# Two decoder blocks of two layers each: layer loops written out, one weight queue through the program, norm weights loaded once

## What is computed

```python
for l in range(2):                                    # first_block, "A"
    h = rmsnorm(x, g_mix[l])
    (cq, ckv, kr, aq, ak, av, qi, ki, wi, rq, rk, rv, rg) = split(h @ w_in[l])
    ...                                               # latent, sparse and retention attention
    x = x + concatenate([o_a, o_b, o_c]) @ w_out[l]
    x = x + square(relu(rmsnorm(x, g_mlp[l]) @ w_ff1[l])) @ w_ff2[l]
x = rmsnorm(x, g_final)
for i in range(2):                                    # second_block, "B"
    (...) = split(rmsnorm_2(h, ln_mix[i]) @ w_in[i])
    ...                                               # delta rule, sparse and stick-breaking attention
    h = h + mix @ w_out[i]
    h = h + conv_ffn(rmsnorm_2(h, ln_ffn[i]), w_up[i], ffn_conv[i], w_down[i])
    gate = sigmoid(rmsnorm_2(h, ln_ple[i]) @ w_ple_gate[i])
    h = h + gate * rmsnorm_2(p[i] @ w_ple[i], ple_norm[i])
return rmsnorm_2(h, ln_final)
```

## Time and profile before

| | |
|---|---|
| time, median of 3 runs | 3295.99 us |
| runs | 3292.2, 3295.99, 3296.8 us |
| span of the profiled execution | 3298.4 us (its own time outside the profiler is not given) |
| TensorE busy | 3144.2 us, 95% |
| VectorE, ScalarE, GpSimd busy | 55%, 39%, 12% |
| weights read | 234 MB, 72 GB/s over the span |

### The profile page before, as it was taken

How to read it: one execution, slowest core, us unless ns; L and a number is a source line. 1 busy time by engine, 2 the same in 40 slices (tenths; PEclk the granted TensorE clock), 3 DMA queues, 4 the chain that set the end, 5 groups by cost and what they waited for, 6 DMA issues and landing times. The chain is left out here.

```text
span 3298.4 us, 48870 instructions
## 1 busy us (share of the span) xinstructions
PE 3144.2 (95%) x19216; PEld 2651.6 (80%) x19216; DVE 1812.1 (55%) x3220; ACT 1302.5 (39%) x2692; POOL 391.2 (12%) x374
## 2 busy tenths in 40 slices
PE   8999999999999999979999999999899999999996
PEld 6878788877878888868888878888788878788885
DVE  4875443425865424337566457474475565574744
ACT  4454432334354413233374333233443653332324
POOL 1031000001040000001213302010004034010100
PEclk9999999999999999989999999999999999999998
DMA  4111222212202222132100122222222000222230
GB/s 169 55 52 39 90 91 101 90 69 91 74 1 77 90 99 93 51 105 104 65 1 2 40 83 99 91 101 87 73 99 85 1 2 28 83 93 93 93 110 35
DMA packets 37342, 239.55 MB, mean 73 GB/s; under 512 B 4464, under 2 KB 5232, under 8 KB 15088
## 3 DMA queue, kind: packets, MB, share of 16 engines
q1 hardware_dynamic: 36528, 234.21, 20.1%
q10 hardware_dynamic: 576, 2.10, 0.2%
HBM read 234.19 MB, written 2.10 MB: 72 GB/s over the span
## 5 line engine op out<-in xcount | busy, mean ns | idle before, releaser
L265 PE MATMUL ps<-b_hl,bff_whl 128*128 128x512 f32 x704 | 274.1, 389 | 3.1 <-DVE b_hl L667 3.1
L267 PE MATMUL ps<-b_hl,bff_whl 128*128 128x512 f32 x704 | 273.9, 389 | 0.0
L266 PE MATMUL ps<-b_hl,bff_whl 128*128 128x512 f32 x704 | 273.9, 389 | 0.0
L248 DVE SCALAR_TENSOR_TENSOR bff_whl<-ring,b_cols,bff_whl 128x512 fp32r<-128x512 f32 (+1 forms) x224 | 153.2, 745 | 197.3 <-ACT bff_whl L235 197.1
L245 DVE TENSOR_TENSOR aff_whl<-ring,aff_whl 128x512 fp32r<-128x512 f32 x160 | 99.8, 685 | 222.8 <-ACT aff_whl L233 222.7
L235 ACT ACTIVATE bff_whl<-ring,b_cols 128x512 fp32r<-128x512 f32 (+1 forms) x224 | 136.6, 682 | 176.4 <-PE ps L267 176.4
L266 PE MATMUL ps<-aff_whl,a_u 128*128 128x512 f32 x512 | 204.3, 399 | 0.0
L265 PE MATMUL ps<-a_hl,aff_whl 128*128 128x512 f32 x512 | 199.5, 390 | 3.1 <-DVE a_hl L667 3.1
L265 PE MATMUL ps<-aff_whl,a_u 128*128 128x512 f32 x512 | 201.7, 394 | 0.0
L267 PE MATMUL ps<-aff_whl,a_u 128*128 128x512 f32 x512 | 200.7, 392 | 0.0
L267 PE MATMUL ps<-a_hl,aff_whl 128*128 128x512 f32 x512 | 199.2, 389 | 0.0
(11 more groups left out here) (524 smaller groups left out, 7746.5 us busy)
## 6 DMA issues: line engine op xcount, KB each, us to landing
ring<-in_a_w_ff SPq DMA_DIRECT2D x64, 1024.0 KB, 4.6
ring<-in_b_w_up SPq DMA_DIRECT2D x32, 1024.0 KB, 4.7
ring<-in_a_w_in SPq DMA_DIRECT2D x16, 1024.0 KB, 5.9
ring<-in_b_w_down SPq DMA_DIRECT2D x16, 1024.0 KB, 4.6
ring<-in_b_w_in_att SPq DMA_DIRECT2D x12, 1024.0 KB, 4.7
ring<-in_b_w_up SPq DMA_DIRECT2D x16, 768.0 KB, 4.0
ring<-in_b_w_in_conv SPq DMA_DIRECT2D x12, 768.0 KB, 4.2
ring<-in_a_w_out SPq DMA_DIRECT2D x8, 1024.0 KB, 4.8
```

Of the source, the lines that this page charges most:

```text
L248: self.c.nc.vector.scalar_tensor_tensor(out=self.part(j, 1, k), in0=src[:, k, :], scalar=g[:, row + k:row + k + 1], in1=self.part(j, 0, k) ...
L265: nc.tensor.matmul(bank, sh, mh, start=start, stop=False)
L266: nc.tensor.matmul(bank, sh, ml, start=False, stop=False)
L267: return nc.tensor.matmul(bank, sl, mh, start=False, stop=stop)
```

## The change

Both loops are written out: each layer is a call of `first_layer` or `second_layer` with a constant l, and every tile's name carries the layer's tag. `start_layer` and `end_layer` go. `queue_layer` appends all chunks of the four layers to one queue, whose addresses are constants, and the four slots' semaphores count through the program; `may_load` bounds how far SP may load: in A up to the third chunk of B, since the fourth slot holds the final gain (`c.ring` is then that slot), in B to the end. So the last stage of a layer loads the first four chunks of the next one (three from A to B). `end_weights` clears the five semaphores once, at the end, with no barrier. The norm gains of both A layers are loaded once, and so are the columns and rows of both B layers (one DMA for the columns and one per layer for the rows); only `g_ret` is still loaded in each A layer, and nothing in that stage waits for it but SP at its end. The 40 idle transposes at the end of `aff` and of `LayerTail` go. In `LayerTail` ScalarE's final squares are placed between the last sigmoids. In the last norm of all, ScalarE's squares are left out (nobody reads them). The stages themselves stay as they are. The core of the diff:

```diff
+    def queue_layer(self, weights, drams, prefix, l):
+        at = {}
         for name, chunks in weights:
             for k, kt, n, w in chunks:
-                self.queue.append((drams[prefix + name], (k, kt, n, w)))
-                self.offsets.append(at.get(name, 0))
...
+                o = at.get(name, 0)
+                self.queue.append((drams[prefix + name][l:l + 1, :, o:o + kt * w], (k, kt, n, w)))
+                at[name] = o + kt * w
     def load_up_to(self, sp, end, first=0, slot_read=None):
-        for i in range(self.loaded, min(end, len(self.queue))):
+        end = min(end, self.may_load)
+        for i in range(self.loaded, end):
...
-    def end_layer(self):
-        nc = self.nc
+    def end_weights(self):
         assert self.used == self.loaded == len(self.queue)
-        nc.all_engine_barrier()
         for s in self.slot_full + [self.chunk_used]:
-            nc.sync.sem_clear(s)
-        nc.all_engine_barrier()
+            self.nc.sync.sem_clear(s)
@@ make_hi
-        if j >= 2:
+        if self.first + j >= 2:
             act.wait_ge(self.c.chunk_used, self.first + j - 1)
@@ projections_a
-                small_loads(sp, arrived)
+                if first_loads is not None:
+                    first_loads(sp, arrived)
+                late_load(sp, late_here)
                 w.load(sp)
-                sp.wait_ge(arrived, 32)
+                sp.wait_ge(late_here, 16)
...
-                act.wait_ge(arrived, 32)
+                if first_loads is not None:
+                    act.wait_ge(arrived, 16)
@@ projections_b
-                small_loads(sp, arrived)
+                if loads is not None:
+                    loads(sp, arrived)
                 w.load(sp)
-                sp.wait_ge(arrived, 32)
...
-                act.wait_ge(arrived, 32)
+                if n_loads:
+                    act.wait_ge(arrived, 16 * n_loads)
@@ out_and_feed_forward
-                pe.wait_ge(down1_added, 1)
-                c.stay_busy(pe, 0, 40)
@@ LayerTail
-        pe.wait_ge(self.gated, 1)
-        self.c.stay_busy(pe, 0, 40)
...
+    def end_square(self, act, t):
+        act.wait_ge(self.done, TT + t + 1)
+        act.wait_ge(self.squares, 2 * TT + t)
+        self.c.nc.scalar.activation(self.junk, self.x[:, t, :], ACT.Square, accum_out=self.c.x_ssq[:, t:t + 1]
+                                    ).then_inc(self.squares, 1)
...
             for t in range(TT):
                 self.sigmoid(act, n, t)
-        for t in range(TT):
-            act.wait_ge(self.done, TT + t + 1)
...
+                if n and t:
+                    self.end_square(act, t - 1)
+        self.end_square(act, TT - 1)
@@ rows_norm
             def _(act):
+                if c.used == len(c.queue):
+                    return
@@ first_block
-    with nc.Fori(0, layers) as l, ExitStack() as ctx:
-        c.start_layer(A_WEIGHTS, d, "a_", l)
...
-        c.end_layer()
+    for l in range(layers):
+        c.queue_layer(A_WEIGHTS, d, "a_", l)
+    after = len(c.queue) + RING - 1
+    for l in range(layers):
+        c.queue_layer(B_WEIGHTS, d, "b_", l)
+    c.may_load = after
...
+        def load_gains(sp, arrived):
+            sp.dma_start(all_gains[:], d["a_gains"][0:layers].rearrange("l p n -> p l n")).then_inc(arrived, 16)
+
+        def load_ret(sp, arrived, l):
+            sp.dma_start(g_ret[:], d["g_ret"][l:l + 1, :].broadcast_to([P, RET_H * RET_D])).then_inc(arrived, 16)
+        for l in range(layers):
+            c.tag = f"_{l}"
+            first_layer(c, all_gains[:, l, :], g_ret, (cos32, sin32, cos64, sin64), decay, half,
+                        load_gains if l == 0 else None, lambda sp, arrived, l=l: load_ret(sp, arrived, l))
+    c.ring = c.slots[:, after % RING:after % RING + 1, :]
@@ second_block
-        with nc.Fori(0, layers) as l, ExitStack() as ctx:
...
+        def small_loads(sp, arrived):
+            sp.dma_start(all_cols[:], d["b_cols"][0:layers].rearrange("l p n -> p l n")).then_inc(arrived, 16)
+            for l in range(layers):
+                sp.dma_start(all_rows[:, l, :], d["b_rows"][l:l + 1, 0:B_NROWS].broadcast_to([P, B_NROWS])
                              ).then_inc(arrived, 16)
...
+        c.may_load = len(c.queue)
+        for l in range(layers):
+            c.tag = f"_{l}"
+            second_layer(c, d, l, {n: all_cols[:, l, a:b] for n, (a, b) in B_COLS.items()},
+                         {n: all_rows[:, l, a:b] for n, (a, b) in B_ROWS.items()}, half, cos, sin, pos_i,
+                         (small_loads, layers + 1) if l == 0 else (None, 0))
+    c.end_weights()
```

More of the change, by code:

```diff
@@ L142, in sb, with tile @@
         return self.ctx.enter_context(self.nc.sbuf_tensor(name, shape, dt))
+    def tile(self, name, shape, dt=F32, **where):
+        return self.nc.sbuf_tensor(name + self.tag, shape, dt, **where)
     @contextmanager
@@ L216, in __init__ @@
             self.tiles.append(self.tiles[-1] + kt)
-        self.buf = ctx.enter_context(core.nc.sbuf_tensor(name + "whl", [P, 2, 2, CHUNK], F32R, side="right"))
+        self.buf = ctx.enter_context(core.tile(name + "whl", [P, 2, 2, CHUNK], F32R, side="right"))
         core.used += n_chunks
@@ L1040, with projections_a @@
 SEARCH_EARLY = 15
-def projections_a(c, hl, gains, half, proj, q, kcat, cos32, sin32, scratch, score, best, small_loads):
+def projections_a(c, hl, gains, half, proj, q, kcat, cos32, sin32, scratch, score, best, first_loads, late_load):
     nc = c.nc
@@ L1408, in projections_b @@
         norm = sb("norm", [P, TT, 2 * GDN_H])[:]
+        loads, n_loads = small_loads
         with c.stage("bin", "hi", "lo", "meaned", "rooted", "rows", "x_turned", "x_his", "x_los",
@@ new lines, in first_block @@
+    for l in range(layers):
[4 more added lines that the diff above has]
+    c.may_load = after
+    with ExitStack() as ctx:
+        all_gains = ctx.enter_context(c.tile("a_gains", [P, layers, 24]))
+        g_ret = ctx.enter_context(c.tile("a_g_ret", [P, RET_H * RET_D]))
+        def load_gains(sp, arrived):
[6 more added lines that the diff above has]
+                        load_gains if l == 0 else None, lambda sp, arrived, l=l: load_ret(sp, arrived, l))
@@ new lines, in second_block, with second_layer @@
+        c.may_load = len(c.queue)
[5 more added lines that the diff above has]
+    c.end_weights()
+def second_layer(c, d, l, cols, rows, half, cos, sin, pos_i, small_loads):
+    split_tile = lambda ctx: ctx.enter_context(c.tile(f"b_hl{c.n_stage}", [P, 2, 8, SEQ], F32R, side="right"))
+    with ExitStack() as left, ExitStack() as right:
+        mix = left.enter_context(c.tile("b_mix", [P, TT, DM], F32))
+        with ExitStack() as mid:
+            sbm = lambda n, s: mid.enter_context(c.tile("b_" + n, s, F32))
+            zab, qkv = sbm("zab", [P, TT, B_ZAB]), sbm("qkv", [P, TT, GDN_QKV])
+            g = {n: sbm("g_" + n, [P, TT, GDN_H])[:] for n in ("beta", "gcum", "minus_g", "eg", "el", "etot")}
+            with ExitStack() as inner:
+                proj = inner.enter_context(c.tile("b_proj", [P, TT, B_ATT], F32))
+                hl = split_tile(right)
+                with c.tile("b_sT", [P, 4, SEQ], F32) as sT:
+                    projections_b(c, hl, cols, rows, half, proj, zab, qkv, g, sT, mix, cos, sin, pos_i, small_loads)
+                right.close()
+                attentions(c, proj, mix, rows, cols, half)
+            gated_delta(c, mix, zab, qkv, g, rows, half)
+        hl = split_tile(right)
+        left.close()
+        F = B_HALF // P
+        with ExitStack() as last:
+            sb1 = lambda n, s, dt=F32: last.enter_context(c.tile("b_" + n, s, dt))
+            sb1("shift", [P, 8])
+            u = sb1("u", [P, 2, F, SEQ], F32R)
+            acc, silus = sb1("acc", [P, 4, SEQ]), sb1("silus", [P, F, SEQ])
+        with ExitStack() as last:
+            sb1 = lambda n, s, dt=F32: last.enter_context(c.tile("b_" + n, s, dt))
+            sb1("shift2", [P, 8])
+            ple, ple_row = sb1("ple", [P, TT, DM]), sb1("ple_row", [P, DM])
+            sb1("under_acc", [P, 2 * F * SEQ - (TT + 1) * DM + 4 * SEQ])
+            pT = sb1("pT", [P, 2, D_PLE // P, SEQ], F32R)
+            sb1("under_silus", [P, F * SEQ - 2 * D_PLE // P * SEQ])
+            out_and_conv_feed_forward(c, mix, hl, cols, rows, half,
+                                      d["p"][l:l + 1].rearrange("a p t n -> p (a t) n"),
+                                      u, acc, silus, ple, pT, ple_row,
+                                      d["b_rows"][l:l + 1, B_NROWS:].broadcast_to([P, DM]))
```

318 lines of the change are left out of this document (130 added, 188 removed).

## The result

The changed kernel takes **3247.85 us** (median of 4 runs, 3245.85 to 3249.02) against 3296.39 beside it; the ratio is 0.9851, interval 0.9839 to 0.9862. The profiled execution has a span of 3244.9 us and a time of 3246.72.

What follows compares the result with a forecast made beforehand. The prediction took TensorE's stream, busy 95% of the span, as the bound, winnable where it stops or runs at the lower clock. Four terms summed to 30.9 us off the median 3296.0, giving 3265.1, range 3259 to 3275 or 3276.

Steps and rivals of the forecast that it cites:

- The joins: The four places where a layer ends: 10.6 + 3.4 + 13.0 + 3.9 = 30.9 us to be gained.
- A to A: Between A's two layers: no idle transposes, loop branch or clock fall, first product 10.6 us earlier, bounds 6.4 and 10.8.
- second chain: Between A's layers, ScalarE's path through the weight tiles, with the chunk already in its slot, to 717.4.
- B to B: Between B's two layers: squares 2.0, start without loop or chunk wait 10.2, clock 0.8; sum 13.0, bounds 11.5 and 14.5.
- The squares: At the ends of B's layers: moving the squares of x between the sigmoids ends the last one 2.0 us earlier.
- The last stages: From B to the end: squares 2.0, fewer clears and barriers 0.6, last norm without ScalarE's squares 1.3; sum 3.9 us.
- A to B: From A's last layer to B's first: final gains' DMA 3.1 us earlier, chunk present at B's start 0.3; together 3.4.
- Costed at nothing: Effects priced at zero: constant DMA addresses, extra waits on used chunks, prefetched chunks' transfers, and 176 KB more of early column loads.
- Rival (1): The clock falls at A to A and B to B: gains 6.4 and 12.2, total gain 25.9, 3270.1 us; chance 0.15.
- Rival (2): A stage beginning far away in the code stalls TensorE 3.6 us even without a branch: gain 23.5, 3272.5 us; chance 0.10.
- Rival (3): Slower: written-out second layers are never-run code and TensorE stalls at their pages, up to 284 us, 3549; chance 0.02.
- Rival (4): Nothing measurable changes, because a later wait takes back what is won; chance 0.03.

Runs made afterwards that it cites:

- busy_back: The changed kernel with both groups of 40 idle transposes put back at the layer ends, nothing else; 3256.46 us, ratio 0.9878.
- u_moved: The kernel before, loops kept, with only spacer tiles lengthened so the down products' stationary tile lies at the changed kernel's address residues; 3281.58 us, ratio 0.9954.
- scan1: The changed kernel with different spacers in each layer, putting the down products' stationary tile at other address residues; one run, 3262.82 us.
- loop_alone: The kernel before with its layer loops written out and no semaphore clears between layers; idle transposes, barriers, no prefetch and late squares kept; 3293.83 us, ratio 0.9991.

## Why the prediction was wrong

**The joins: right.** Their four terms were forecast at 30.9 and came to 32.6. In A to A the 2.45 of the transposes, TensorE's start 0.3 behind the last work, the idle of 2.3 (2.22), the clock at 1.00 and the 3.6 us of transposes (3.69) all stand in the rows; only the last step, the first product, was 0.38 earlier behind ScalarE than forecast. That is the forecast's second chain: it let ScalarE begin on the weights 3.2 us behind its end, and it began 1.93 behind (707.68 - 705.75), since the load of its activation table (1.28) is not there in the written-out code. The first product came 0.25 ahead of the transposes' last end, before (728.19) as after (709.74), which points to the transposes as what set it.

Two things in these sums were luck. The clock that stays up at A to A was taken from one stage boundary at 260, where it held through an idle of 2.09. The same boundary in layer 1 of the same trace, at 966.00, has the same idle, and there the clock fell (0.50 over 966.2 to 969.5); the forecast did not use that row:

```profile
966.00 4.12 PE L2464 MATMUL ps<-a_rqT,a_rkT 64*128 64x512 f32 x16 [2.09 <-PEq L151]
```

Over the 14 profiled executions it fell at this boundary in 5 of 28 places, and at A to A in 2 of 10. And at B to B the 13.2 is near the 13.0 because two misses nearly cancel: the forecast gave 0.8 for a clock that might stay up, and it fell (`busy_back` prices that at 1.7), while the rest, 10.2 without the clock, came to 11.1. Part of that is likely that layer 0's stage, with which it was compared, had run its first 5.3 us at 1.2 GHz, more than the 4.3 that the forecast took. The squares' 2.0 were 2.1. The last stages and A to B were within 0.9.

**The failed step** is that the sum has terms for the four joins alone. The stages between them were taken to run as before, and the paragraph "Costed at nothing" lists registers, waits, chunks and the bytes of the small loads, but not the tiles that these loads fill. Both layers' gains and columns lie in SBUF at once, so these tiles are larger, and every tile behind them has another address. The prediction took an address to be without cost. `u_moved` shows that it is worth 14.4 us by itself, with none of the rest. There were two signs of it before: on the page three matmul lines with the same form and no wait ahead of them had means of 399, 394 and 392, while the up products stood at 389 and 390, and the source had spacer tiles that nothing uses. The range failed with it, since each of its bounds was a bound of a join, with only the runs' spread added.

**Rival (1), the clock falls in both places:** half right. It fell at B to B (0.57), which the forecast had left open, and not at A to A (1.00), as forecast, in the changed kernel's two profiled executions. The Trainium skill, "TensorE: Matmul & The Clock Gate", Part 1, says that recent activity releases the throttle; the traces agree, for the clock fell behind every idle of 3.67, 4.14 and 7.08 us, and held through 2.22 in eight executions of ten. Taking the transposes out of A cost nothing in the eight and 1.5 us in `scan1`, of the 2.45 that it earned; in B it cost 1.66 us at one join and earned 1.0 there.

**Rival (2), a stall wherever the code goes far:** wrong. TensorE's start is 0.30 behind the last work at A to A and at B to B of the changed kernel. **Rival (3), stalls in code not run before:** wrong. `loop_alone` has the written-out code and the old rest and is at 0.9991. **Rival (4), a later wait takes it back:** wrong for the whole change, but right for its first part alone: in `loop_alone` at A to A the chunk and the clock took back all but 0.2 us.

**The parts do not add.** `loop_alone` is 3.5 us faster than before, within what can be told, and without the prefetch the changed kernel loses some 14. Stall, chunk and clock lay beside each other at A to A: with one gone, the next sets the time. The forecast followed both chains to the first product in place of adding up the waits, which is why it was near here although one chain was sized wrong.

## What to carry to other kernels

Ask of a change that adds or enlarges an on-chip tile which tiles move with it, and compare the matmuls' durations by form: equal forms with unequal means and no idle time are a hint of placement, and a spacer tile of some bytes tests it in one run. Here the two tiles of a product wanted a distance of 0 modulo 256 bytes. When you take "the clock stays up" from one row, look at every place with the same idle before you do. Where a stall, a transfer and a low clock lie in one gap, follow each chain to the first useful instruction: removing one of them alone may bring nothing, as the written-out loops did.

## What the runs showed of the hardware

- The step of a float32r matmul of 128x128 by 128x512 depends on the distance from its moving to its stationary tile in SBUF modulo 256 bytes: 226.7 ns at 0, 229.1 at 192, 232.4 at 128, 233.3 to 234.4 at the five others tried (32, 64, 96, 160, 224). Residues alone do not decide (224 and 224 are as fast as 128 and 128).
- At the joins the granted clock stayed at 1.00 behind an idle of 2.22 us in eight executions and fell to 1.2 GHz for 3.4 us in two. It fell behind 3.67 in all eight executions that have it (3.4 us), behind 4.14 (3.4 us) and with 7.08 (10.2 us).
- A pair of barriers of all engines with nothing between them put TensorE's start 1.9 (A to A) and 3.4 us (B to B) later than the stage's own barrier.
- Stretches of 3.4 us at 1.2 GHz come and go between executions and kernels at places with 1.6 to 2.1 us of idle (the norm ahead of the up products, as at 356 us in `busy_back` and not in the changed kernel; the boundary at 260 and 966 us). They cost 0.6 to 1.9 us each in their stages. What decides was not tried.
